# The levels of a packed triangular inverse: masked product against a whole block-diagonal stationary, growing product in 64x64 tiles, key transposes moved forward

## What is computed

```python
kk = jnp.einsum("bhncd,bhnmd->bhncm", k, k)
a_mat = jnp.where(strict, kk * beta[..., :, None] * decay, 0.0) + jnp.eye(c)   # c = 64
rhs = jnp.concatenate([v * beta[..., None], k * (beta * jnp.exp(gc))[..., None]], axis=-1)
sol = lax.linalg.triangular_solve(a_mat, rhs, left_side=True, lower=True, unit_diagonal=True)
u, w = sol[..., :dv], sol[..., dv:]
```

## Time and profile before

| | us |
|---|---|
| median of 3 runs | 3367.1 |
| lowest and highest run | 3359.89, 3370.2 |
| the profiled execution, its own time | 3360.2 |
| its span | 3358.4 |
| PE busy in the span | 3236.4 (96%) |
| DVE, ACT, POOL busy | 1562.8, 1118.9, 345.2 |
| mean granted TensorE clock | 0.981 |

### The profile page before, as it was taken

How to read it: one execution, slowest core, us unless ns; L and a number is a source line. 1 busy time by engine, 2 the same in 40 slices (tenths; PEclk the granted TensorE clock), 3 DMA queues, 4 the chain that set the end, 5 groups by cost and what they waited for, 6 DMA issues and landing times.

```text
span 3358.4 us, 46279 instructions
## 1 busy us (share of the span) xinstructions
PE 3236.4 (96%) x20080; PEld 2626.7 (78%) x20080; DVE 1562.8 (47%) x2484; ACT 1118.9 (33%) x1806; POOL 345.2 (10%) x584
## 2 busy tenths in 40 slices
PE   7898999999999999999999999999999899999999
PEld 5686878887887788887876577888887786767886
DVE  5646354444433544355136644433444427554444
ACT  6456332212444422222235533211112336432222
POOL 1202000000210010001000104100001301030000
PEclk9899899999999999999999999999999999999999
DMA  3111022422226332222325331222012213013321
GB/s 133 52 51 52 26 76 84 142 76 88 79 101 245 107 117 97 76 76 71 91 95 186 101 101 51 76 76 76 18 59 70 58 45 95 26 51 113 113 76 38
DMA packets 190747, 281.88 MB, mean 84 GB/s; under 512 B 19144, under 2 KB 122184, under 8 KB 190416
## 3 DMA queue, kind: packets, MB, share of 16 engines
q1 hardware_dynamic: 188368, 272.19, 24.2%
q10 hardware_dynamic: 2176, 6.73, 0.6%
HBM read 273.66 MB, written 2.10 MB: 82 GB/s over the span
## 4 chain that ended last, share of the span: by engine, by line
PE 88%; DVE 4%; ACT 4%; POOL 2%; issue 2%; DMA 1%; ACTq 0%; DVEq 0%; POOLq 0%; SPq 0%
PE ps L825 11%; PE ps L827 11%; PE ps L826 11%; PE ps L543 6%; PE ps L544 6%; PE ps L545 6%; PE ps L856 5%; PE ps L857 5%; PE ps L858 5%; PE ps L439 3%; PE ps L618 2%; PE ps L619 2%; PE ps L620 2%; PE ps L1451 2%; PE ps L1419 2%
## 5 line engine op out<-in xcount | busy, mean ns | idle before, releaser
L448 ACT ACTIVATE R<-ring 128x2048 fp32r<-128x2048 f32 (+4 forms) x285 | 401.6, 1416 | 1003.4 <-PE ps L827 353.0
L825 PE MATMUL ps<-R,R 128*128 128x512 f32 (+1 forms) x1760 | 651.8, 370 | 8.8 <-DVE R L1314 4.1
L827 PE MATMUL ps<-R,R 128*128 128x512 f32 (+1 forms) x1760 | 649.2, 369 | 0.0
L826 PE MATMUL ps<-R,R 128*128 128x512 f32 (+1 forms) x1760 | 649.2, 369 | 0.0
L543 PE MATMUL ps<-R,R 128*128 128x512 f32 (+1 forms) x1016 | 398.3, 392 | 21.4 <-DVE ringlo L639 10.6
L825 PEld LDWEIGHTS ps<-R,R 128*128 128x128 f32 x1760 | 332.6, 189 | 70.0 <-DVE R L1314 4.8
L544 PE MATMUL ps<-R,R 128*128 128x512 f32 (+1 forms) x1016 | 382.1, 376 | 0.0
L545 PE MATMUL ps<-R,ringlo 128*128 128x512 f32 (+1 forms) x1016 | 381.3, 375 | 0.0
L827 PEld LDWEIGHTS ps<-R,R 128*128 128x128 f32 x1760 | 332.6, 189 | 55.4
L826 PEld LDWEIGHTS ps<-R,R 128*128 128x128 f32 x1760 | 332.5, 189 | 54.5
L761 DVE TENSOR_TENSOR R<-ring,R 128x2048 fp32r<-128x2048 f32 x88 | 203.8, 2317 | 304.5 <-ACT R L448 304.4
(11 more groups left out here) (317 smaller groups left out, 4479.1 us busy)
## 6 DMA issues: line engine op xcount, KB each, us to landing
ring<-in_w_mod SPq DMA_DIRECT2D x24, 2048.0 KB, 9.3
ring<-in_ffn_w_in SPq DMA_DIRECT2D x44, 1024.0 KB, 12.0
ring<-in_w_ffn_in SPq DMA_DIRECT2D x44, 1024.0 KB, 12.2
ring<-in_ffn_w_out SPq DMA_DIRECT2D x10, 2048.0 KB, 7.9
ring<-in_w_ffn_out SPq DMA_DIRECT2D x10, 2048.0 KB, 7.7
ring<-in_dil_w_in SPq DMA_DIRECT2D x9, 2048.0 KB, 7.7
ring<-in_gdn_w_in SPq DMA_DIRECT2D x8, 2048.0 KB, 8.8
ring<-in_w_in SPq DMA_DIRECT2D x6, 1536.0 KB, 9.3
```

Source lines behind the costliest of these rows:

```text
L448: return act.e.activation(o, i, fn, **kw)
L825: pe.e.matmul(ps, w[0], x[0], start=(k == 0), stop=False)
L826: pe.e.matmul(ps, w[0], x[1], start=False, stop=False)
L827: t = pe.e.matmul(ps, w[1], x[0], start=False, stop=(k == 7))
```

## The change

- The masked product takes the four diagonal 32x32 blocks of a matrix as one 128x128 stationary, AD, zero elsewhere: 8 matmuls of 32 columns for 32. AD fills `bufs[6]`; GpSimd zeroes it and copies the blocks in (two memsets, eight copies), and TensorE's masks wait for those copies. The zeroing of T64, which lies in the same place, moves behind the last mask.
- The growing product takes two quarters at once: 64x64 stationary tiles, 16 matmuls for 32. For that `dve_masked` writes each result twice, 512 elements for each partition instead of 256, with masks GP that keep each copy in its own half. XP moves within its buffer, the constants grow from 352 to 448 columns.
- The four key turns stand ahead of the second small product, the first value turn ahead of the first mask, the second one in level 2, and ScalarE's and VectorE's lists are put in the same order.

```diff
-        tg_const = arena(0, 352)
-        GM, TRI = arena(0, 7, 32), arena(224, 128)
+        tg_const = arena(0, 448)
+        GM, GP, TRI = arena(0, 2, 32), arena(64, 4, 2, 32), arena(320, 128)
...
-        XP, X5 = arena(bufs[7] + 1024, 2, 8, 32), arena(bufs[7] + 1536, 2, 8, 32)
+        XP, X5 = arena(bufs[7] + 1024, 16, 2, 32), arena(bufs[7] + 1536, 2, 8, 32)
+        AD = arena(bufs[6], 2, 8, 128)
...
             pe_small(hg, 0)
+            for c in range(4):
+                pe_keys_turned(hg, c)
             pe_small(hg, 1)
-            pe_keys_turned(hg, 0)
-            pe_keys_turned(hg, 1)
+            pe_values_turned(hg, 0)
             pe_masked(hg, 1, 0)
-            pe_keys_turned(hg, 2)
             pe_masked(hg, 1, 1)
-            pe_keys_turned(hg, 3)
             pe_grown(hg, 1, 0)
             pe_grown(hg, 1, 1)
             for n in range(2, 5):
                 pe_masked(hg, n, 0)
                 pe_masked(hg, n, 1)
-                if n < 4:
-                    pe_values_turned(hg, n - 2)
+                if n == 2:
+                    pe_values_turned(hg, 1)
                 pe_grown(hg, n, 0)
                 pe_grown(hg, n, 1)
...
         def pe_masked(hg, n, g):
             ps = bank("mask", hg, n, g)
             pe.wait_ge(*at("t", hg, n - 1, g))
+            for i in range(4):
+                pe.wait_ge(*at("a block", hg, g, i))
             for b in range(8):
-                for r in QU:
-                    t = pe.e.matmul(ps[r, 32 * b:32 * b + 32], AB[r, g, b, r], TP[r, g, 0, b, :], start=True, stop=True)
+                t = pe.e.matmul(ps[:, 32 * b:32 * b + 32], AD[:, g, b, :], TP[:, g, 0, b, :], start=True, stop=True)
...
             for b in range(8):
-                for r in QU:
-                    t = pe.e.matmul(ps[r, 32 * b:32 * b + 32], XP[r, g, b, :], TP[r, g, 1, b, :], start=True, stop=True)
+                for r in (slice(0, 64), slice(64, 128)):
+                    t = pe.e.matmul(ps[r, 32 * b:32 * b + 32], XP[r, 8 * g + b, :, :].rearrange("p a b -> p (a b)"),
+                                    TP[r, g, 1, b, :], start=True, stop=True)
...
             z = z_pieces(hg)
+            act_values_weighed(hg, 0)
             act_split(z[0], WHZ[hg])
-            act_values_weighed(hg, 0)
+            act_values_weighed(hg, 1)
             act_split(z[1], WHZ[hg])
-            act_values_weighed(hg, 1)
...
             dve_keys_tailed(hg, 1)
+            dve_grown(hg, 1, 0)
             dve_keys_tailed(hg, 2)
-            dve_grown(hg, 1, 0)
             dve_grown(hg, 1, 1)
+            dve_keys_tailed(hg, 3)
             for n in range(2, 5):
                 dve_masked(hg, n, 0)
                 dve_masked(hg, n, 1)
-                if n == 2:
-                    dve_keys_tailed(hg, 3)
...
             dve.wait_ge(*at("mask", hg, n, g))
-            dve.e.tensor_tensor(XP[:, g], by_block(PS.of("mask", hg, n, g))[:, 0],
-                                GM[:, n + 1:n + 2, :].broadcast_to([128, 8, 32]), M).then_inc(
+            dve.e.tensor_tensor(XP[:, 8 * g:8 * g + 8],
+                                by_block(PS.of("mask", hg, n, g))[:, 0].unsqueeze(2).broadcast_to([128, 8, 2, 32]),
+                                GP[:, n - 1].unsqueeze(1).broadcast_to([128, 8, 2, 32]), M).then_inc(
...
             pool_heads(hg, 12)
-            pool.wait_ge(*at("ps", "kq", hg, 3))
-            pool.e.memset(T64[0:32, :, :, 32:64], 0.0).then_inc(*pool.done("t zero", hg))
+            for g in range(2):
+                if g:
+                    pool.wait_ge(*at("a block", hg, 0, 3))
+                pool.wait_ge(*at("ps", "kq", hg, 2 * g + 1))
+                pool.e.memset(AD[:, g], 0.0).then_inc(*pool.done("a zero", hg, g))
+                pool.wait_ge(*at("a zero", hg, g))
+                for i, r in enumerate(QU):
+                    pool.e.tensor_copy(AD[r, g, :, r], AB[r, g, :, r]).then_inc(*pool.done("a block", hg, g, i))
+            pool.wait_ge(*at("a block", hg, 1, 3))
             pool.wait_ge(*at("k turned", hg, 3))
             pool.e.memset(k_, 0.0).then_inc(*pool.done("tt zero", hg))
             pool.wait_ge(*at("tt zero", hg))
+            pool.wait_ge(*at("mask", hg, 4, 1))
+            pool.e.memset(T64[0:32, :, :, 32:64], 0.0).then_inc(*pool.done("t zero", hg))
```

More of the change, by code:

```diff
@@ L32 @@
 K_GDN = K_RES
-N_GDN = 7 * 32 + 128 + 512
+N_GDN = 10 * 32 + 128 + 512
 K_DIL = K_GDN + N_GDN
@@ L57, in constants @@
     g = K_GDN
-    low, up = i % 32, np.arange(32)[None, :]
-    for n, r, c in ((0, low, up), (0, up, low), (1, low, up), (2, low, up), (3, low, up), (4, low, up)):
+    up = np.arange(32)[None, :]
+    k[:, g:g + 32] = i % 32 == up
+    k[:, g + 32:g + 64] = (i % 32 // 2 == up // 2) & (i % 2 == 0) & (up % 2 == 1)
+    g += 64
+    for n in range(1, 5):
         b = 1 << n
[L61 to L64, removed]
+        z, w = i % 64, np.arange(64)[None, :]
+        k[:, g:g + 64] = (z // (2 * b) == w // (2 * b)) & (z % (2 * b) >= b) & (w % (2 * b) < b)
+        g += 64
     k[:, g:g + 128] = i <= j
@@ L1696, in act_boot @@
             act.e.dma_start(KC[:, :], a["kc"][:, 0:K_RES]).then_inc(*lane("kc").done("kc"))
-            act.e.dma_start(tg_const, a["kc"][:, K_GDN:K_GDN + 352]).then_inc(*lane("gm").done("gm"))
-            act.e.dma_start(res, a["kc"][0:8, K_GDN + 352:K_GDN + 864]).then_inc(*lane("res").done("res"))
+            act.e.dma_start(tg_const, a["kc"][:, K_GDN:K_GDN + 448]).then_inc(*lane("gm").done("gm"))
+            act.e.dma_start(res, a["kc"][0:8, K_GDN + 448:K_GDN + 960]).then_inc(*lane("res").done("res"))
             act.wait_ge(*at("col"))
@@ L2386, in dve_small @@
             dve.wait_ge(*at("ps", "small", hg, g))
-            dve.e.tensor_tensor(TP[:, g, 1], GM[:, 6:7, :].broadcast_to([128, 8, 32]), TP[:, g, 1], SUB).then_inc(
+            dve.e.tensor_tensor(TP[:, g, 1], GM[:, 0:1, :].broadcast_to([128, 8, 32]), TP[:, g, 1], SUB).then_inc(
                 *dve.done("tt", hg, 0, g))
```

## The result

The changed kernel took 3392.3 us (median of 4 runs, 3390.9 to 3398.0), the kernel before 3366.2 beside it (4 runs, 3359.9 to 3370.2): a ratio of 1.0081, 95% interval 1.0066 to 1.0096. It is slower by 26 us. The forecast was 3396, range 3368 to 3408.

The account below looks back on a forecast made before the run. The levels were taken to wait for instructions, at a low clock. With the change, TensorE-bound levels of 10.9 us (masks, growing, switches) add 15.9 and 13.4 us in the two passes: 3396 on the median, range 3368 to 3408.

Parts of the forecast that it names:

- Masks, 3.4 us a group at the low clock: Masked product in the levels: 16 records with 128-column loads at 0.21 us each, 3.4 us a group at 1.2 GHz.
- The choice between 0.11 and 0.21: Cost in us of one 128-column weight load at 1.2 GHz; 0.21 taken, since the load's own duration grows by 141 ns.
- Rival B: Full-width load costs 0.11 us at either clock: level 7.7 us, kernel 3371, no change; chance 0.08.
- Growing, 1.75: Growing product in the levels: two 64x64 tiles side by side, 16 x 0.11 = 1.75 us a group at the low clock.
- rival C: The two 64x64 tiles of growing groups don't run side by side: +28 us on top, 3424; chance 0.05.
- Shape switches, 0.6 us a level: TensorE's loads wait 0.33 us where tile shapes change; a level switches twice, 0.6 us.
- The clock, low from the first masks on: TensorE at 1.2 GHz from the first masks to L2110, since masks mostly load and stream only 32 columns.
- VectorE, GpSimd: Level work beside TensorE: masked product 0.68 us for 0.42; two memsets, eight copies of 0.3 to 0.35 us; cost nothing.
- The price named for a lost cover: If mask (1, 0) didn't hold TensorE long enough to hide GpSimd's copies for g = 1: 1 us a pass.
- The statement that the key tails end before TensorE gets there: VectorE's key tails (0.68 us each) free banks for level 1's growing and level 2's masks before TensorE needs them.
- The sum: Second pass +15.9 us (45.4 against 29.5), first +13.4, together +29.3: 3389.5 on the profiled execution, 3396 on the median.
- Rival A: The clock holds at 2.4 GHz through the levels: level 5.9 us, four with ends 25.0, kernel 3345, faster; chance 0.15.

Follow-up runs that it names:

- run 1: Changed kernel with each mask matmul streaming 64 columns for 32, the added half not read: 3374.3 us, ratio 1.0018.
- run 9: Changed kernel with each mask group in two 64x64 tiles side by side (32 records, 64-column loads) for one 128x128: 3366.1 us, ratio 0.9998.
- run 2: Kernel before with the block-diagonal 128x128 masks alone (AD, its memsets and copies), growing in 32x32 tiles, old order: 3380.8 us, ratio 1.0044.
- run 3: Changed kernel with the old masks (32 matmuls of 32x32, no GpSimd copies), 64x64 growing and new order kept: 3360.2 us, ratio 0.9976.
- run 5: Changed kernel with both mask and growing matmuls streaming 64 columns for 32, the added half not read: 3350.4 us, ratio 0.9961.
- run 10: Changed kernel with masks in two 64x64 tiles, and masks and growing groups both streaming 64 columns: 3338.7 us, ratio 0.9919.

## Why the prediction was right

The direction, the mechanism and the size hold. Two terms of the sum were too large, and part of the nearness of 3396 to 3392 is luck.

- *Masks, 3.4 us a group at the low clock:* measured 3.5 (two in 6.97, 344.72 to 351.69), loads of 333 ns, one per 0.22 us. The choice between 0.11 and 0.21 was right, and runs 1 and 9 show that it is the load and not the stream. Rival B fell with it. The Trainium skill ("TensorE: Matmul & The Clock Gate", section "LDWEIGHTS (loading the stationary operand)") gives 107 ns for 128 columns without a word of the clock; the trace agrees at 2.4 GHz and shows twice that at 1.2.
- *Growing, 1.75:* two groups in 3.55, so 1.78; the tiles run side by side, and rival C fell.
- *Shape switches, 0.6 us a level: this term was too large.* Two growing groups begin to end take 3.55 us here, between masks of another shape (351.69 to 355.24), and 3.41 in run 9, where masks and growing groups have the same shape (149.15 to 152.56). So a switch costs at most 0.14 us, some 0.3 us a level, and a level is 10.52 us for the forecast's 10.9. The 0.33 us of the earlier trace rows were the wrong price for it. In the changed kernel the growing loads wait that long where they follow transposes and not where they follow masks, though both are 128x128:

```profile
341.16 3.49 PEld L2205 LDWEIGHTS ps<-U 64*64 64x64 f32 x64 [0.33 <-issue]
351.68 3.49 PEld L2205 LDWEIGHTS ps<-U 64*64 64x64 f32 x64
```

In run 2, where transposes give way to 128x128 masks, there is no wait either (the loads of the one end at 131.48, those of the other start at 131.46). So the 0.33 us stand only where small tiles follow transposes, which happens once in these levels; why, no run shows. The Trainium skill's rule ("TensorEngine Tiling (Array Packing)", section "Key Properties"), by which a change of tiling mode drains TensorE, isn't contradicted, but the drain is short: at most 0.14 us here.
- *The clock, low from the first masks on: right in kind, late in place.* In the first pass the new order did what was forecast (masks 1.1 us sooner against the small product, 1.2 expected) and the clock fell at 134.4. In the second pass it fell at 328.9, behind level 1's masks, where the forecast had it low from their start. Level 1's two mask groups took 4.0 instead of 7.0 us: 3.0 us of the second pass's overestimate of 4.35 (45.4 against 41.05). The rest is about four times the 0.38 us between 10.9 and 10.52. In the first pass the masks had 2.7 us at 2.4 GHz (131.70 to 134.4), where the forecast counted 1.5, so it cost 11.4 for 13.4.
- *VectorE, GpSimd:* 0.69 us a masked product, hidden. GpSimd's copies took 0.44 to 0.46 each, not 0.30 to 0.35, and were done at 327.34, in time. The price named for a lost cover, 1 us a pass, was 0.6 in runs 9 and 10. The statement that the key tails end before TensorE gets there holds only while the masks are slow: in runs 1, 3, 5, 9 and 10 levels 1 and 2 wait 0.2 to 0.45 us for them.
- *The sum:* +29.3 forecast, +22.3 measured in the two passes, +26 in the medians. The forecast of 3396 is 4 us above the median, nearer than the two passes would bring it (7 us too much). The upper end of the range doesn't follow from its own working: 3396 and 3.5 us for each pass make 3403, not 3408. The measured time lies below either.
- *Rival A* had the right price for the levels (four with ends in 25.0 us; in run 5 the pairs start 25.6 us behind the first mask, 130.91 to 156.50) and nearly for the kernel (3345; run 5 took 3350.4). Its condition didn't come about in the changed kernel: behind loads of 128 columns with 32 streamed the clock fell in both passes, and with 64 streamed for each load (run 5) it stayed high in both.

## What to carry to other kernels

Before packing small blocks into one wide stationary with zeros, compare columns loaded with columns streamed. At 1.2 GHz the masked product of one matrix took 0.44 us on a 128x128 stationary (7.0 / 16), 0.21 in two 64x64 tiles (3.4 / 16) and 0.13 in four 32x32 tiles (2.1 / 16). All three load 128 columns for each matrix; the smaller tiles load them side by side. Look at the granted clock in and behind the stretch as well as at busy time: here a TensorE recorded busy for 97% of 38 us ran at half speed, and streaming more columns that nobody reads brought the other half back. Where waits for instructions are the complaint, the form with the fewest instructions need not be the best. Of the three with 64 streamed columns, the fewest instructions took 3350.4 us (128x128 masks), the most 3345.8 and 3348.9 (32x32, with waits for instructions left), the middle form 3338.7 (64x64). The first two can't be told apart, the last is clear of both.

## What the runs showed of the hardware

- With twice the streamed columns in the level matmuls, and the same loads, TensorE stayed at 2.4 GHz through eight levels (1.00 in both windows of run 5, 0.50 in the changed kernel from level 1 on), and the kernel was about 40 us faster.
- A 128-column f32 load is 192 ns long and begins every 0.11 us at 2.4 GHz, 333 ns and every 0.22 us at 1.2. Two 64-column loads side by side begin within 0.11 us at 1.2 GHz (223 ns each).
- With 64 streamed columns a 64x64 group takes 1.04 us at 2.4 GHz (run 10), with 32 columns at 1.2 GHz 1.7 to 1.8 (run 9, changed kernel).
- Loads of 64x64 or 32x32 tiles waited 0.33 us behind 128x128 transposes at 1.2 GHz; behind 128x128 matmuls the loads of 64x64 tiles waited less than 0.1.
- With 256 pairs of load and multiply a level, TensorE waited at steps of 128 pairs, 3.9 us apart; with 96 the levels have no such wait.
- The executions of run 1 differ by 35 us, those of run 9 by 3.5. The mean clocks go with them: 0.975 to 0.986 in run 1, 0.978 and 0.979 in run 9.
